# Rows of summed decays in the SSD layer: broadcast by DMA from memory in place of products on TensorE

## The reference, cut to what matters

```
acum_h[t]  = cumulative sum over the chunk of dt_h[t] * a_h        # the "summed decays"
L_h[s, t]  = exp(acum_h[t] - acum_h[s])   for s <= t, within and across the two chunks
y_h[t]     = sum over s of (C[t] . B[s]) * L_h[s, t] * dt_h[s] * x_h[s]
```

## Time and profile before

| | |
|---|---|
| profiled execution, its own time | 3574.1 us |
| its span, first to last instruction | 3572.3 us |
| median of the three runs | 3571.8 us |
| mean granted clock of TensorE | 0.995 |
| TensorE busy (products) | 3504.6 us, 98% |
| VectorE busy | 2225.8 us, 62% |
| ScalarE busy | 1597.9 us, 45% |
| GpSimd busy | 589.7 us, 17% |
| read from memory | 613.75 MB |

### The profile page before, as it was taken

One profiled execution on the slowest core, in us unless ns is written; L12 is line 12 of the kernel. 1 busy time (PEld: TensorE's weight loads), 2 busy tenths in 40 slices (PEclk: granted clock), 3 DMA queues, 4 the chain that ended last, 5 costly groups with the idle time before them and its releaser, 6 DMA issues.

```text
span 3572.3 us, 45011 instructions
## 1 busy us (share of the span) xinstructions
PE 3504.6 (98%) x18462; PEld 2912.5 (82%) x18462; DVE 2225.8 (62%) x2152; ACT 1597.9 (45%) x1764; POOL 589.7 (17%) x528
## 2 busy tenths in 40 slices
PE   7999999999999999999999999999999999999998
PEld 6777888888887777888888878888888888788886
DVE  5667646464655666646464658866576575775676
ACT  4555433333344555434343445633444444553553
POOL 1231000000000221000000001650000079540540
PEclk9999999999999999999999999999999999999999
DMA  6444555555555344555555544455444454345443
GB/s 208 142 153 160 181 188 187 188 189 188 187 183 190 133 165 150 184 187 188 188 188 188 199 177 165 179 188 186 156 143 153 164 183 174 140 154 188 161 159 140
DMA packets 89887, 618.45 MB, mean 173 GB/s; under 512 B 10256, under 2 KB 12560, under 8 KB 16496
## 3 DMA queue, kind: packets, MB, share of 16 engines
q1 hardware_dynamic: 83952, 601.99, 47.1%
q0 software_dynamic: 3168, 11.41, 1.0%
q10 hardware_dynamic: 2592, 2.55, 0.2%
HBM read 613.75 MB, written 2.10 MB: 172 GB/s over the span
## 4 chain that ended last, share of the span: by engine, by line
PE 90%; DVE 4%; ACT 2%; issue 1%; DMA 1%; POOL 1%; DVEq 0%; SPq 0%; ACTq 0%; POOLq 0%
PE ps L2272 27%; PE ps L2274 14%; PE ps L2230 7%; PE ps L2231 7%; PE ps L2232 7%; PE ps L2328 2%; PE ps L2685 2%; PE ps L2686 2%; PE ps L2687 2%; PE ps L2304 2%; PE ps L2305 1%; PE ps L2306 1%; DVE wlo L1374 1%; PE ps L2367 1%; PE ps L2369 1%
## 5 line engine op out<-in xcount | busy, mean ns | idle before, releaser
L2272 PE MATMUL ps<-act,whi 128*128 128x512 f32 x4384 | 1551.1, 396 | 1.9 <-DVE wlo L1367 1.8
L2274 PE MATMUL ps<-act,wlo 128*128 128x256 f32 x4384 | 1233.7, 281 | 0.0
L1367 DVE TENSOR_TENSOR wlo<-raw,whi 128x2048 fp32r<-128x2048 f32 x404 | 941.2, 2350 | 468.0 <-ACT whi L926 445.8
L2272 PEld LDWEIGHTS ps<-act,whi 128*128 128x128 f32 x4384 | 824.1, 188 | 202.8 <-issue 8.4
L926 ACT ACTIVATE whi<-raw 128x2048 fp32r<-128x2048 f32 x358 | 683.6, 1913 | 616.6 <-DMA raw<-in_w_down 309.9
L2274 PEld LDWEIGHTS ps<-act,wlo 128*128 128x128 f32 x4384 | 822.8, 188 | 0.5
L818 ACT ACTIVATE whi<-raw 128x2048 fp32r<-128x2048 f32 x212 | 404.4, 1913 | 279.0 <-DMA raw<-in_o_w_in 113.8
L1374 DVE TENSOR_TENSOR wlo<-raw,whi 128x2048 fp32r<-128x2048 f32 x166 | 393.4, 2374 | 160.4 <-ACT whi L818 160.4
L2230 PE MATMUL ps<-whi,act 128*128 128x512 f32 x1152 | 455.7, 396 | 0.0
L2231 PE MATMUL ps<-wlo,act 128*128 128x512 f32 x1152 | 455.2, 395 | 0.0
L2232 PE MATMUL ps<-whi,act 128*128 128x512 f32 x1152 | 455.1, 395 | 0.0
(11 more groups left out here) (393 smaller groups left out, 4502.8 us busy)
## 6 DMA issues: line engine op xcount, KB each, us to landing
raw<-in_w_up SPq DMA_DIRECT2D x128, 1024.0 KB, 4.8
raw<-in_w_down SPq DMA_DIRECT2D x128, 1024.0 KB, 4.8
raw<-in_o_w_in SPq DMA_DIRECT2D x80, 1024.0 KB, 4.8
raw<-in_e_w_in SPq DMA_DIRECT2D x64, 1024.0 KB, 4.8
raw<-in_w_in SPq DMA_DIRECT2D x60, 1024.0 KB, 4.8
raw<-in_w_o SPq DMA_DIRECT2D x32, 1024.0 KB, 4.8
raw<-in_e_w_out SPq DMA_DIRECT2D x32, 1024.0 KB, 4.8
raw<-in_o_w_out SPq DMA_DIRECT2D x32, 1024.0 KB, 4.8
```

Of the source, the lines that this page charges most:

```text
L1367: dve.tensor_tensor(wlo[:, slot, :], raw[:, slot, :], whi[:, slot, :].bitcast(F32), ALU.subtract).then_inc(sem("lo_ready"), 1)
L2272: pe.matmul(ps[:, b + f, :], whi[:, slot, w], a[:, kt, :, :].rearrange("p a t -> p (a t)"), start=(kt == 0), stop=False)
L2274: ins = pe.matmul(ps[:, b + f, S:2 * S], wlo[:, slot, w], a[:, kt, 0, :], start=False, stop=(kt == KT - 1))
```

## The change

The rows no longer go through TensorE. `decays` is written once to memory, as a tensor of 64 x 256 (64 KB), by GpSimd's queue in place of the copy within SBUF. From there ScalarE's queue fetches, before each half of a group, two transfers of two heads' rows each (2 KB), repeated on 128 partitions (256 KB each), into two SBUF areas (`osq` and a part of `std`). VectorE's minimum and ScalarE's first exponential read them there in place of PSUM. The calls of `decay_rows` are gone from TensorE. A fetch is issued when ScalarE has done the exponentials that read the area before.

```
-        decay_halves = [cos[0:DH, :], cos[up, :]]
+        decay_out = nc.dram_tensor("decay_rows", (N_SSD_H, S), F32, kind="Internal").ap()
+        decay_rows = [osq[:, :, :].rearrange("p a t -> p (a t)"), stdf[:, S:3 * S]]
...
-                            pool.dma_start(cos[0:DH, :], cos[up, :]).then_inc(sem("d_both"), 16)
+                            pool.dma_start(decay_out, decays).then_inc(sem("d_out"), 16)
...
+            def decay_fetch(g, first):
+                wait(act, sem("s_w"), 4 * g + first // 2)
+                for par in range(2):
+                    h = 8 * g + first + 2 * par
+                    act.dma_start(decay_rows[par], decay_out[h:h + 2].rearrange("(a e) t -> a (e t)", a=1).broadcast_to(
+                        [P, 2 * S])).then_inc(sem(f"d_in{par}"), 16)
...
-                        a = ps[:, 4 + pair % 2, e * S + P:e * S + 2 * P]
+                        a = decay_rows[pair % 2][:, e * S + P:e * S + 2 * P]
...
+                        if s.get("pre") == "bc" and g == 6:
+                            act.wait_ge(sem("d_out"), 16)
+                            decay_fetch(0, 0)
...
                     high_unit(u + 8)
+                    decay_fetch(g, 4)
                     high_unit(u + 9)
                     decay_exps(g, 4)
                     conv_sigmoid(10 + 2 * g)
+                    decay_fetch(g + 1, 0)
                     conv_sigmoid(11 + 2 * g)
...
                     decay_exps(g, 0)
                     high_unit(u + 6)
+                    decay_fetch(g, 4)
                     high_unit(u + 7)
...
-                    dve.wait_ge(sem("s_a"), 8 * g + first + 4)
+                    dve.wait_ge(sem(f"d_in{pair % 2}"), 16 * (2 * g + pair // 2 + 1))
...
-                                      ps[:, 4 + pair % 2, :].rearrange("p (e c t) -> p e c t", e=2, c=2),
+                                      decay_rows[pair % 2].rearrange("p (e c t) -> p e c t", e=2, c=2),
...
                 wait(pe, sem("s_g"), g)
+                wait(pe, sem("s_cbm"), g)
+                wait(pe, sem("s_xdt"), 2 * g)
...
-            def decay_rows(g, first):
-                pe.wait_ge(sem("d_both"), 16)
...
-                        pe.matmul(ps[:, 4 + par, i * S:i * S + S], ident[rows, at:at + 1].broadcast_to([DH, P]),
-                                  decay_halves[par], start=True, stop=True).then_inc(sem("s_a"), 1)
...
                     products(s, 0, 1, act0)
-                    decay_rows(g, 0)
                     products(s, 1, 0, act0)
                     head_outputs(g, 0)
-                    decay_rows(g, 4)
                     products(s, 1, 1, act0)
```

More of the change, by code:

```diff
@@ L2771, in _ @@
                             ssd_bases(g)
-                        if i == 3:
-                            decay_rows(g, 0)
                         if i == 5:
                             head_outputs(g, 0)
-                            decay_rows(g, 4)
                         if i == 7:
```

## The result

The changed kernel took 3582.9 us (median of 8 runs, 3575.4 to 3586.4); the kernel before took 3574.6 beside it (8 runs, 3571.8 to 3576.1). The ratio is 1.0023, with an interval of 1.0014 to 1.0033: 8 us slower, a little over the 7.1 that I took as what a measurement of this kernel can tell, and 0.9 beyond the upper end of my range (3582). The forecast was 2 us slower.

A forecast was written before the change was run, and what follows sets the result against it. Two equally long chains, TensorE's and one through ScalarE and VectorE, were taken to bound the SSD stages. Terms -2.5 - 0.4 + 1.2 + 2.4 + 0.8 + 0.6 = +2.1 us gave 3574 us, range 3565 to 3582.

The forecast's parts named there:

- Two chains of equal length: Load of u+7 to products(1,1): TensorE's calls and a ScalarE/VectorE chain take the same time; 0.2 us won in g = 1, 4.
- `ssd_out` gave its 2.5: In ssd_out two calls leave TensorE with nothing else due first; both come off, -2.5 us.
- The exponentials cost 0.2 a stage: First-half exponentials reading SBUF instead of PSUM lengthen the second chain: 0.2 in six stages, +1.2 us.
- the minima held GpSimd's pair: VectorE's minima with two SBUF inputs delay GpSimd's convolution beside them: 0 to 1.1 us a stage, 0.4 taken, +2.4.
- the two full minima of 0.68: By the skill's port rule, two minima would hold GpSimd for their full 0.68 us each.
- The fetch of the second half was in time: In g = 2 fetched data is there by 3143.6, before the minimum at 3143.99: hidden by 0.4 us.
- the step that lets the idle time which the calls leave cost nothing: In the SSD stages removed calls become TensorE idle time, 2.3 us in two pieces; the sum charges nothing for it.
- "TensorE's clock falls": Rival: idle time in the SSD stages drops TensorE to 1.2 GHz, 1.7 us a fall; three falls +7.2 us; chance 0.11.
- The prediction's own sign of being wrong: Wrong if the granted clock has more than the few falls of before in the SSD stages.
- Its two reference points in the earlier trace: 0.56 us of TensorE work in 3.30 was followed by 1.2 GHz for 3.4 us; 1.93 in 3.70 stayed at 2.4.
- the wait for the squares of g = 0: The 6.8 us TensorE wait, ended by GpSimd's chain behind exponentials (+0.2) and beside second minima (+0.6): +0.8 us.
- those after g = 3 and g = 6: TensorE's other two waits for the squares, behind second-half exponentials 0.2 longer: 0.3 taken each, +0.6 us.

The follow-up runs named there:

- the kernel before with the swaps: Kernel before, rows still on TensorE; ScalarE's first-half exponentials ahead of the high part of u+7, alone 3571.0 us; second-half ones also ahead of u+9's, 3568.4 us.
- the fill kernel: Changed kernel plus the old row products, unread, in TensorE's idle time after products(1,0) in the seven ssd stages, none in ssd_out: 3576.4 us, 1.0006.
- The second profile of the change: The changed kernel unchanged, measured again beside the experiments against the kernel before: 3580.1 us, ratio 1.0019.

## Why the prediction was wrong

What held. Two chains of equal length: the calls are covered by the second one, and waits of TensorE (18.0) stand where their 17.6 us were. When both chains were shortened the distance fell to 13, and with TensorE's alone (the change) or ScalarE's alone (the kernel before with the swaps) it did not. `ssd_out` gave its 2.5: from the start of the g = 6 products(1,1) to the end it is 1.75 us less (125.40 to 123.65), with one clock window more there (+1.4) and the wait of 0.69 for the squares gone. The exponentials cost 0.2 a stage, and the minima held GpSimd's pair for 0.9. The Trainium skill, page "SBUF — State Buffer", section "SBUF: two separate sides", has that rule. The trace agrees in kind (1.97 and 1.98 against 1.09 and 1.08), not with the two full minima of 0.68 that the prediction made of it: one operation of the pair is held, the other is not. The fetch of the second half was in time.

What failed. First, the step that lets the idle time which the calls leave cost nothing. The sum has no term for the clock; "TensorE's clock falls" stands only among the rivals, at 0.11. What the runs showed in its place: five windows of 3.41 us at 0.50 in the stages, 6.9 us in the profile, and 3.8 to 6.6 us of the median time, by the kernel in which a fill took them away. The prediction's own sign of being wrong, more falls than before in the SSD stages, came true. Its two reference points in the earlier trace rows were about as far from the case as each other: 0.56 us of work in 3.30 with a fall, 1.93 in 3.70 without. The case itself, 1.25 in 3.50, lay between them, and there both outcomes occur. I gave it one chance in nine where the rows favoured neither side. Its price was over-sized: 1.7 a window forecast, about 1.4 measured.

Second, a size: 0.2 and 0.4 us a stage for exponentials and port, less 0.4 won in all, makes +3.2 over six stages; measured +4.6. I had let the convolution meet VectorE's work in three stages of six. It met it in five: the product with C.B in three, the low part behind it in two, each 0.6 to 0.9 longer. That the fill kernel ends at +2.2, next to the forecast's +2.1, is in part luck: the distances there are +4.0 over six stages where the forecast had +3.2.

The profiled executions, 3574.1 and 3584.6 us, differ by 10.5. Of this 2.7 lies ahead of products(1,1) of g = 0, 2.6 of it ahead of the SSD stages, where TensorE's work is the same. The second profile of the change reached that point 0.6 earlier than the kernel before, so I take it as no part of the change. Distances +4.6, clock +6.9, the wait for the squares of g = 0 +0.8, those after g = 3 and g = 6 -1.2 (TensorE comes later by the fall just before; without falls, in the fill kernel, they are 1.5 against 1.2 before; the forecast was +0.6), `ssd_out` -2.5: 8.6, against 7.8 measured from that point to the end; 0.8 is not assigned.

## What to carry to other kernels

Before taking work off a busy engine, look for a second chain of the same length between the same two points; if there is one, the stretch gets shorter only when both do. Here taking off TensorE's alone left the distance no shorter and lost 8 us, and shortening ScalarE's alone left the distance as it was (its 5.7 us came from other waits). Even both together gave nothing while the fetches went out just ahead of a load that sets the pace; with the fetches earlier and the second exponentials moved too they gave 14 us. Idle time that a removal leaves on TensorE is not free: if rows of the trace don't exclude a fall of the clock behind it, give that the weight of a likely case, or fill the idle time. And a transfer beside a load that sets the pace should go out behind that load, or well before it.

## What the runs showed of the hardware that I had not expected

The granted clock fell to 0.50 (1.2 GHz) behind two idle pieces of 0.5 to 1.4 and 1.4 to 2.3 us, 2.7 to 2.9 together, with 0.97 to 1.60 us of work in the 3.5 us ahead of the fall: in nine of ten stages of the two profiles of the change. In the tenth, which looks the same, it did not; nor did it in g = 4, where the pieces are 2.2 and 2.0 together. Two fetches of 256 KB, issued 0.2 to 1.0 us ahead of a load of 1 MB, lengthened that load from 4.8 to between 6.9 and 8.3 us (5.6 in one case of thirty). Issued behind it they themselves took 4.9 to 5.8 instead of 3.1 to 4.4 for the first and 4.9 to 6.8 for the second, and the load 4.7 to 5.5. The Trainium skill, page "DMA: Bandwidth & Descriptors", section "Queues, rings and completion order", has the engines take turns between the queues packet by packet, which fits that each lengthens the other; that the order of issue decides by so much no run here explains.
